# Large matmuls with the moving operand and the accumulator walked from the last column to the first

## The reference

```
x = x + gla_mixer(rms_norm(x, gla_attn_norm[i]), gla_w_in[i], ...)      # h @ w_in ... @ w_out
...
k_shared, v_shared = shared_kv(x, kv_norm, w_kv, k_norm)
x = x + diff_attention(rms_norm(x, diff_attn_norm[j]), k_shared, v_shared, diff_w_q[j], ...)
...
x = x + swiglu(rms_norm(x, ffn_norm[l]), ffn_w_in[l], ffn_w_out[l])     # both layers

def swiglu(h, w_in, w_out):
    g, u = jnp.split(h @ w_in, 2, axis=-1)
    return (jax.nn.silu(g) * u) @ w_out
```

## Time and profile before

| | |
|---|---|
| median of 3 runs | 2193.34 us |
| the profiled execution, its own time | 2193.63 us |
| its span, first to last instruction | 2191.8 us |
| TensorE matmul busy | 2185.7 us, 9732 instructions |
| TensorE weight load busy | 1811.1 us |
| VectorE busy | 1249.6 us |
| ScalarE busy | 1058.1 us |
| GpSimd busy | 283.0 us |
| HBM read | 414.37 MB, 190 GB/s over the span |

### The profile page before, as it was taken

One profiled execution on the slowest core, in us unless ns is written; L12 is line 12 of the kernel. 1 busy time (PEld: TensorE's weight loads), 2 busy tenths in 40 slices (PEclk: granted clock), 3 DMA queues, 4 the chain that ended last, 5 costly groups with the idle time before them and its releaser, 6 DMA issues.

```text
span 2191.8 us, 27280 instructions
## 1 busy us (share of the span) xinstructions
PE 2185.7 (100%) x9732; PEld 1811.1 (83%) x9732; DVE 1249.6 (57%) x1472; ACT 1058.1 (48%) x1432; POOL 283.0 (13%) x563
## 2 busy tenths in 40 slices
PE   9999999999999999999999999999999999999999
PEld 7888888888888888888888888888888888888887
DVE  5666666645555555554566676665555555555443
ACT  6666455444444444444456665554444444444333
POOL 3210334100000000001125333341000000000000
PEclk9999999999999999999999999999999999999999
DMA  8766667676667666666667666677676767666665
GB/s 263 211 187 178 192 201 222 204 217 200 202 206 206 205 204 207 199 201 202 205 198 217 198 207 205 201 224 210 196 211 200 216 193 209 204 211 194 192 194 165
DMA packets 252674, 447.01 MB, mean 204 GB/s; under 512 B 27664, under 2 KB 41968, under 8 KB 252592
## 3 DMA queue, kind: packets, MB, share of 16 engines
q1 hardware_dynamic: 236176, 428.79, 65.1%
q0 software_dynamic: 16240, 17.07, 2.6%
q10 hardware_dynamic: 176, 0.07, 0.0%
HBM read 414.37 MB, written 2.10 MB: 190 GB/s over the span
## 4 chain that ended last, share of the span: by engine, by line
PE 99%; DMA 0%; SPq 0%; DVE 0%; issue 0%
PE acc L655 32%; PE acc L654 32%; PE acc L653 32%; PE acc L665 1%; PE acc L670 0%; PE side L905 0%; DMA x<-in_x 0%; PE tps L692 0%; PE side L741 0%; PE side L776 0%; PE side L903 0%; PE side L919 0%; PE side L921 0%; PE side L920 0%; PE side L792 0%; PE side L791 0%
## 5 line engine op out<-in xcount | busy, mean ns | idle before, releaser
L1343 DVE TENSOR_TENSOR w_lo<-raw,w_hi 128x1024 fp32r<-128x1024 f32 x784 | 953.9, 1223 | 809.4 <-ACT w_hi L966 805.3
L966 ACT ACTIVATE w_hi<-raw 128x1024 fp32r<-128x1024 f32 x784 | 826.0, 1059 | 981.7 <-PE acc L655 972.6
L653 PE MATMUL acc<-w_hi,xT 128*128 128x512 f32 x2016 | 786.3, 390 | 0.0
L655 PE MATMUL acc<-w_hi,xT 128*128 128x512 f32 x2016 | 784.4, 389 | 0.0
L654 PE MATMUL acc<-w_lo,xT 128*128 128x512 f32 x2016 | 784.3, 389 | 0.0
L655 PEld LDWEIGHTS acc<-w_hi,xT 128*128 128x128 f32 x2016 | 378.4, 188 | 78.7
L653 PEld LDWEIGHTS acc<-w_hi,xT 128*128 128x128 f32 x2016 | 378.4, 188 | 78.5
L654 PEld LDWEIGHTS acc<-w_lo,xT 128*128 128x128 f32 x2016 | 378.4, 188 | 78.3
L653 PE MATMUL acc<-w_hi,hT 128*128 128x512 f32 x700 | 272.3, 389 | 0.0
L654 PE MATMUL acc<-w_lo,hT 128*128 128x512 f32 x700 | 272.3, 389 | 0.0
L655 PE MATMUL acc<-w_hi,hT 128*128 128x512 f32 x700 | 272.3, 389 | 0.0
(11 more groups left out here) (207 smaller groups left out, 1386.4 us busy)
## 6 DMA issues: line engine op xcount, KB each, us to landing
raw<-in_ffn_w_in SPq DMA_DIRECT2D x352, 512.0 KB, 4.2
raw<-in_ffn_w_out SPq DMA_DIRECT2D x176, 512.0 KB, 4.7
raw<-in_gla_w_in SPq DMA_DIRECT2D x96, 512.0 KB, 4.3
raw<-in_w_kv SPq DMA_DIRECT2D x64, 512.0 KB, 4.3
raw<-in_gla_w_out SPq DMA_DIRECT2D x32, 512.0 KB, 4.5
raw<-in_diff_w_q SPq DMA_DIRECT2D x32, 512.0 KB, 5.0
raw<-in_diff_w_out SPq DMA_DIRECT2D x32, 512.0 KB, 4.9
tok<-scratch SPq DMA_DIRECT2D x352, 32.0 KB, 3.2
```

Of the source, the lines that this page charges most:

```text
L653: nc.tensor.matmul(acc[p][tb][:, :], hi, w_hi[:, slot, j, :], start=(kt + j == 0), stop=False)
L655: last = nc.tensor.matmul(acc[p][tb][:, :], lo, w_hi[:, slot, j, :], start=False, stop=(kt + j == n_kt - 1))
L966: nc.scalar.activation(w_hi[:, slot, :, :], raw[:, slot, :, :], ACT.Copy).then_inc(hi_done, 1)
L1343: nc.vector.tensor_tensor(w_lo[:, slot, :, :], raw[:, slot, :, :], w_hi[:, slot, :, :].bitcast(F32), ALU.subtract).then_inc(lo_done, 1)
```

## The change

In the three matmuls of `unit` the free dimension of the accumulator and of the moving operand is indexed with `::-1`. Element 511 of both is taken first and element 0 last. The stationary operand, the flags, the waits and the order of the instructions are as before, and so are `first_unit`, `last_unit` and whatever reads the accumulators.

```diff
-                        nc.tensor.matmul(acc[p][tb][:, :], hi, w_hi[:, slot, j, :], start=(kt + j == 0), stop=False)
-                        nc.tensor.matmul(acc[p][tb][:, :], hi, w_lo[:, slot, j, :], start=False, stop=False)
-                        last = nc.tensor.matmul(acc[p][tb][:, :], lo, w_hi[:, slot, j, :], start=False,
+                        nc.tensor.matmul(acc[p][tb][:, ::-1], hi, w_hi[:, slot, j, ::-1], start=(kt + j == 0), stop=False)
+                        nc.tensor.matmul(acc[p][tb][:, ::-1], hi, w_lo[:, slot, j, ::-1], start=False, stop=False)
+                        last = nc.tensor.matmul(acc[p][tb][:, ::-1], lo, w_hi[:, slot, j, ::-1], start=False,
                                                 stop=(kt + j == n_kt - 1))
```

## The result

The changed kernel takes 2255.18 us (median of 4 runs, 2254.61 to 2255.2) against 2193.66 us for the kernel before, measured beside it (4 runs): a ratio of 1.0279, with a 95% interval of 1.0266 to 1.0292. It is slower by 61.5 us. That lies within the stated range of 2188 to 4190 us, but it is neither the likeliest case of the prediction, which was no change, nor the doubling that held most of the rest.

What follows compares the result with a forecast made beforehand. TensorE, never waiting after the start, was taken to bound the kernel through 9300 large matmuls at 0.227 us. The change's sum was 9300 x 0 = 0 us, giving 2193.5 us, range 2188 to 4190 us (forecast's own 2189 to 2198).

Steps and rivals of the forecast that it cites:

- one nanosecond is 9.3 us and 0.4%: In the 9300 large matmuls: each nanosecond added per matmul lengthens the kernel by 9.3 us, or 0.4%.
- the two doublings: In every matmul of `unit`: backward write or backward read costs a second cycle per column, 4080 to 4178 us; together 0.38.
- its two cases: For the whole kernel: no difference, 2193.5 us, chance 0.52, or the two doublings, 4080 to 4178 us, chance 0.38.
- I take zero: In the 9300 large matmuls: a step of -1 adds nothing to the pace, 9300 x 0 = 0 us.
- The backward write at a second cycle per column: First rival, accumulator of every `unit` matmul: results go in singly, 1888 to 1984 us more, 4080 to 4178 us; chance 0.24.
- the backward read likewise: Second rival, at w_hi and w_lo: backward reads fetch neighbours one by one, 4080 to 4178 us; chance 0.14.
- The third rival: At each descending walk's start: small fixed cost per matmul, 1 to 5 ns, 9 to 47 us, 2203 to 2240 us; chance 0.06.
- some ns further apart, and the same ns in xT and hT groups: Sign of a fixed cost per matmul: large matmul starts lie further apart, equally in the xT and hT groups.
- the bound of a gain: In the large matmuls: removing all of the 0.013 us beside the columns would gain 127 us; faster had chance 0.02.
- the fourth rival: In the 9300 large matmuls: a rate such as four cycles per column, 5951 us more, 8145 us; chance 0.02.
- Reading the rule by its reason: For PSUM writes: lines hold two fp32 values, still taken one after the other when reversed, so no change.

Runs made afterwards that it cites:

- e2: Kernel before with only the accumulator write of the three large matmul lines reversed, the moving operand read forward: 2193.53 us, ratio 1.0.
- m2: Second kernel of bare matmul patterns, other block lengths, widths and starts: reversed blocks of 4, 8, 16, 32 took 544, 560, 640, 560 cycles.
- m1: First kernel of bare matmul patterns, no other engine at work, 192 matmuls per section: 512 columns forward 43.56 us, 544 cycles; read reversed 560.
- m4: Kernel of bare matmul patterns, 96 per section, with one or both operand tiles moved: forward in place 21.76 us, moving tile moved by 8 elements 22.40.

## Why the prediction was right and where it was wrong

**What bounds the kernel: right.** TensorE without a wait, 9300 matmuls at a pace, and the change worth 9300 times what it adds to that pace. The measured 61.6 us of span are 9300 x 6.62 ns. The sentence that one nanosecond is 9.3 us and 0.4% was the most useful one: it says in advance how much a few ns of one instruction weigh.

**The number: inside the range by luck.** 2255 us lies in a range that was stretched to 4190 us to take in the two doublings. The forecast itself was 2189 to 2198 us, and the prediction called everything between its two cases unlikely.

**The term that failed: "I take zero".** The step from the rows was that both operands keep the same bytes in the same aligned block and that a step of -1 keeps pairs in the same 8 bytes. For the write this held: it costs nothing in e2. For the read it did not. The bytes and the block were indeed the same, and the read cost 6.6 ns all the same, so the order of the walk matters beyond them. The pairs were not the unit either: up to four elements reversed are free (m2), and eight are not.

**The rivals.** The backward write at a second cycle per column (0.24) and the backward read likewise (0.14) are both wrong: e2 shows nothing, and the read costs 16 cycles per 512 columns and not 512. The plain f32 rows, from which I took the second cycle, belong to another type and were no sign of how a direction behaves; plain f32 itself shows no price for a backward read. The third rival, a small cost per matmul, comes nearest, with the sign in the profile that I gave it ("some ns further apart, and the same ns in xT and hT groups"), and it had 0.06. I priced it at 1 to 5 ns and 2203 to 2240 us; it was 6.6 ns and 2255 us. Its mechanism, a fixed cost at the start of each descending walk, is wrong: the price was 16 cycles at 512 columns, 11 at 384 and none at 320, and eight walks of 64 cost no more than one of 512. I had written that no row speaks for it. One gave a hint: the pace of 0.227 us contains **0.013 us beside one cycle per column**, which I noted and used only as the bound of a gain. In the chain, forward plain f32 matmuls of 256 columns show almost none of it (0.43 us for two instructions of 512 cycles). Something in the fp32r matmul already cost 32 cycles, and it was the place to ask what could make them 48. The runs show that this part varies with the order in which the moving operand is read and with the places of both operands. In the fourth rival I wrote that no TensorE row is as slow as four cycles per column. Each of the two pieces in the earlier trace rows is two instructions at two cycles per column, and in m1 a plain f32 matmul of the code is two such instructions, so a whole product there takes four.

**The Trainium skill's rule.** The rule on PSUM's lines (the Trainium skill, Advanced Engine Details and Errata, section Memory Cachelines) does not hold, by its word "non-contiguous", for a step of -1: the write alone took 2193.53 us. For a step of 2 it does: 256 bf16 columns written with step 2 took 518 cycles against 262. Reading the rule by its reason, lines of two values, was right for the write. What I left out was the same section of the Trainium skill on reads: it states 16-byte lines in SBUF and full performance where one access after another hits the same line. That four reversed fp32 elements are free and eight are not agrees with lines of this size, but the price of the eight, or of a fully backward read, does not follow from it: these too take the four elements of a line one after another, and they cost 16 cycles. The section also asks for at least two hits in a line to absorb the memory's latency; two were not enough here: with step 2 every line is hit twice in a row, and L253 took 1088 cycles and not 544. The page gives no price that would have led to 6.6 ns.

**The signs in the profile.** What I had written for a fixed cost is what the profile shows (mean duration 398 ns on `xT` and on `hT`, where it was 390 and 389), with `last_unit` at its old pace. ScalarE's idle time before L966 grew by 68 us, 64 of them ended by TensorE, and TensorE itself still has no wait behind the start (1.2 and 0.6 us there). The chances were wrong in their weights: I spread 0.38 over two mechanisms with the same price, each a guess at the memory's logic, and gave the mild form of the same effect 0.06.

## What to carry to other kernels

When one engine never waits, price a change per instruction to the nanosecond, and ask of the pace it has now which part is not accounted for by its columns. For fp32r matmuls with 512 columns, that part depends on the order of the read and on where the two operands lie: full 128x128 stationary tiles and moving tiles, both on a multiple of 512 bytes and read forward, gave 544 cycles. Other places and a backward read gave 544 to 568, and some chopped or interleaved walks more. The 16 cycles are 3% of a kernel like this and can be lost by inserting 32 bytes of padding ahead of a tensor. If an order has to be turned, reverse the write and not the read; the write was free here.

## What the runs showed of the hardware

- A backward read of the moving fp32r operand costs 16 cycles of 2.4 GHz at 512 columns (560 against 544), 11 at 384, none at 320, and saves 4 at 256. In bf16 and in plain f32 it costs nothing.
- Direction is not the only thing that brings this price: a forward read moved by 8 elements takes the same 560 cycles (m4, and 2255.32 us for the kernel). Moving the stationary tile by 16 gives 560, moving both by 16 gives 545, but moving both by 4 gives 555. Backward and moved by 16 cost the kernel no more than backward alone (2255.29 us); the moving tile moved by 96 is an exception, 568 cycles backward against 560 forward. Why place and direction matter, and why no fully backward read of 512 columns took fewer than 560 cycles at any place tried, is open; no run looks inside.
- Blocks of 16 elements reversed inside cost 96 cycles per matmul (2565 us for the kernel), blocks of 8, 32 and 64 cost 16, blocks of 2 and 4 nothing (m1, m2). Why 16 is the bad length is open.
- An fp32r read with step 2 takes 2.12 cycles per column (1088 for 512), a bf16 write with step 2 2.02 (518 for 256). A backward write costs nothing.
- At 512 columns no order or place tried brought an fp32r matmul below 544 cycles, 32 beside its columns; at 256 columns the backward read had 28. A bf16 matmul showed 6 beside its columns (262 for 256), and each plain f32 instruction 6 beside two cycles per column (518 for 256).
